# Third norm's mean ahead of its second low parts, turns of the mixed rows four to a slot, high weights first in slots two to four

## The chip, the cores and the metric

The kernel runs on one core of one Trainium2 chip. The metric is the device time of one execution in microseconds (us), lower is better. Before the change it is 2747.4 us (median of three runs, 2747.28 to 2749.04).

## The reference, cut to what matters

256 tokens of width 2048 pass through two blocks, all in float32. The parts of the computation that the change touches:

```python
# start of block one: the first norm feeds the first projection
h = rms_norm(x, mix_pre_g);  proj = h @ w_in          # first columns used: v
# end of block one, start of block two (third norm of the kernel's numbering)
x = x + rms_norm((silu(gate) * up) @ w_ffn_out, ffn_post_g)
h = rms_norm_2(x, norm_mix_pre_2);  z = h @ w_in_2    # first columns used: R0
# block two: the "mixed rows"
gates = sigmoid(gate_logits + b_branch_gates)
mixed = (gates[0] * y_a + gates[1] * (o @ w_branch_b_2)) @ w_out_2
```

## The kernel before, in words

**Two parts of every number.** TensorE multiplies in a reduced float32 form, so every factor is split into a high part (rounded) and a low part (what the rounding left). A product is three matmuls: low tokens times high weights, high tokens times low weights, high times high. Token factors live in `AH`/`AL` and `BH`/`BL` (high/low), the weights of the moment in `RH`/`RL`.

**The weight stream.** The weights come as 964 slots of 128x1024 numbers (512 KB), in the order in which they are used. Slot `i` is loaded by the SP queue into `RAW[i % 4]`; ScalarE copies it to its high part `RH[i % 4]` (line 1166); VectorE subtracts to get the low part `RL[i % 4]` (line 1672); TensorE multiplies with both. Each ring has four places: the high part of slot `i` waits until TensorE is through with slot `i-4`, and the load of slot `i` waits until the low part of slot `i-4` is made. A slot of a product by tokens is 12 matmuls of 512 columns: 2 blocks of 128 input features, 2 halves of the tokens, 3 products. `by_token` writes them; it waits for the slot's low part first (`wait_low`) and then, in the first product that uses new tokens, for the tokens' low parts (`ready`).

**Order of the other work.** Each engine's program is in a fixed order. `upto(i + LA)`, with `LA = 3`, makes the part of slot `i+3` while the engine's program stands at slot `i`. Everything else is a generator that yields the slot at which its next piece is to be written, in halves; `sides.behind(i - 0.5)` and `sides.behind(i)`, behind the part of slot `i+3`, write what is due. So a piece with 3.5 stands behind the part of slot 7 of its count, a piece with 4.5 behind that of slot 8, and what is written later on the same engine waits for it.

**The start.** Slot 0 (`first_slot`) goes by parts: 4 high-high, 4 with low tokens, 4 with low weights. Slots 1 to 7 of the pass `v0` go through `by_token`.

**The third norm** (`n == 3`, pass `R0`). The last product of block one ends by halves of the tokens. In `half_norm` VectorE adds the sum of a half, makes the mean of the squares (`"mean"`, needs ScalarE's squares), GpSimd raises it to the power -1/2, VectorE adds the scaled rows to `X` in quarters (`"first_quarters"` and on). TensorE turns the quarters of `X` (`half_turns`, steps 0 to 7), ScalarE makes the high and VectorE (`half_lows`) the low parts of each step. `by_token_head` mixes these turns with the products of the first four slots of `R0`. Steps 0 and 1 belong to the first half of the tokens, 2 and 3 to the second.

**The mixed rows.** Passes `yb0` to `yb3` (8 slots each) are followed by `W0`, which multiplies the rows that they make. Behind the last slot of each `yb{j}` VectorE takes the product from PSUM (one operation), adds the other branch (one), turns 128x1024 numbers by 16 transposes of 32x256 (line 2151, four for each `fq`); ScalarE makes the high part (`mixed_task`, line 1484), VectorE the low part (`mixed_task`, line 2136 and on). In `W0` the slot numbered 7 from the last of `yb3` is the first to need the low part of `yb3` (`ready` is `(s_ybl, k // 4 + 1)`, two `k` to a slot).

Of the kernel before, what the change touches and what calls it, by code (L numbers as in the profile page):

```python
# [13 lines left out]
P = 128  # L14
# [153 lines left out]
def build(nc, A, out, scratch):  # L168
    ctx = ExitStack()
    with ctx:  # L170
# [87 lines left out]
        def last(name):  # L258
            return groups[name][-1]
# [296 lines left out]

        X_AT = [5, 6, 8, 9]
        X_CHUNK, X_PIECES = [0, 2, 4, 8, 12, 16], [1, 2, 3, 4]
        X_HALF = [(half, b) for half in range(2) for b in range(2)]


# [15 lines left out]
        def tensor(g):  # L577
# [75 lines left out]
            def by_token(name, H, L, ready=None):  # L653


                banks, k = unit[name, 0], 0
                tail = groups[name][-2:] if name == "ckv1" else []
                wait_unit(name)
                for i in groups[name]:
                    if i in tail:  # L660
                        break
                    if i == 0:
                        first_slot(banks, H, L)
                        k = 2
                        sides.behind(i)
                        continue
                    wait_low(i)
                    hi, lo = parts(i)
                    for j in range(2):
                        if ready:  # L670
                            g.wait_ge(*ready(k))
                        end = i == last(name) and j == 1
                        for b in range(2):
                            o, bs = PS[:, banks[b], :], slice(b * P, b * P + P)
                            mm(o, L[:, k, bs], hi[:, j, :], k == 0, False)
                            mm(o, H[:, k, bs], lo[:, j, :], False, False)
                            t = mm(o, H[:, k, bs], hi[:, j, :], False, end)
                        k += 1
                        if j == 0:
                            sides.behind(i - 0.5)  # L680
                    t.then_inc(s_slot, 1)
                    sides.behind(i)
                if tail:
                    for b in range(2):
                        o, bs = PS[:, banks[b], :], slice(b * P, b * P + P)
                        for n, i in enumerate(tail):
                            wait_low(i)
                            hi, lo = parts(i)
                            for j in range(2):
                                c = k + 2 * n + j  # L690
                                mm(o, L[:, c, bs], hi[:, j, :], False, False)
                                mm(o, H[:, c, bs], lo[:, j, :], False, False)
                                t = mm(o, H[:, c, bs], hi[:, j, :], False, n == 1 and j == 1)
                            if b:
                                t.then_inc(s_slot, 1)
                        if b == 0:
                            t.then_inc(s_vh, 1)
# [61 lines left out]
            def by_token_head(name, H, L, n):  # L759

                banks, head = unit[name, 0], groups[name][:4]
                wait_unit(name)

                def highs(b, ms):
                    for m in ms:
                        g.wait_ge(s_nhi, 8 * n + 2 * b + m // 2 + 1)
                        g.wait_ge(s_hi, head[m] + 1)  # L770
                        for j in range(2):
                            mm(PS[:, banks[b], :], H[:, 2 * m + j, b * P:b * P + P], parts(head[m])[0][:, j, :], m + j == 0, False)

                def low_tokens(b, ms):
                    for m in ms:
                        g.wait_ge(s_nlo, 8 * n + 2 * b + m // 2 + 1)
                        for j in range(2):
                            mm(PS[:, banks[b], :], L[:, 2 * m + j, b * P:b * P + P], parts(head[m])[0][:, j, :], False, False)

                def low_weights(b, ms):  # L780
                    for m in ms:
                        wait_low(head[m])
                        for j in range(2):
                            t = mm(PS[:, banks[b], :], H[:, 2 * m + j, b * P:b * P + P], parts(head[m])[1][:, j, :], False, False)
                        if b:
                            t.then_inc(s_slot, 1)
                            sides.behind(head[m])

                highs(0, range(2))
                if n == 3:  # L790
                    low_weights(0, range(2))
                highs(0, range(2, 3))
                low_tokens(0, range(2))
                highs(0, range(3, 4))
                if n == 3:
                    half_turns(n, 2, 3)
                low_tokens(0, range(2, 4))
                if n != 3:
                    half_turns(n, 2, 3)
                    low_weights(0, range(1))  # L800
                half_turns(n, 3, 4)
                if n != 3:
                    low_weights(0, range(1, 2))
                highs(1, range(4))
                low_tokens(1, range(4))
                low_weights(1, range(2))
                half_turns(n, 4, 6)
                low_weights(0, range(2, 4))
                low_weights(1, range(2, 4))
                rest_by_token(name, H, L, n)  # L810
# [350 lines left out]
        def scalar(g):  # L1161
# [321 lines left out]

            def mixed_task():
                for j in range(4):
                    yield last(f"yb{j}") + 3
                    g.wait_ge(s_ybt, j + 1)
                    act(AH[:, 4 * j:4 * j + 4, :], MIXT[j % 2].rearrange("p (c t) -> p c t", c=4)).then_inc(s_ybh, 1)

# [177 lines left out]
        def vector(g):  # L1667
# [74 lines left out]
            def half_norm(n, half):  # L1742


                f = first(NORMED[n])
                for step in ("early", "sum", "mean", "first_quarters"):
                    half(0, step)
                upto(f + (n == 3))
                if n != 3:
                    half(0, "last_gain")  # L1750
                    half(0, "third_quarter")
                    half(0, "last_quarter")
                half(1, "early")
                half(1, "sum")
                half_lows(n, 0, 2)
                if n == 3:
                    half(0, "last_gain")
                half(1, "mean")
                half(1, "first_quarters")
                upto(f + 2)  # L1760
                half_lows(n, 2, 4)
                upto(f + 3)
                if n == 3:
                    half(0, "third_quarter")
                half(1, "third_quarter")
                upto(f + 4)
                half_lows(n, 4, 5)
                half(1, "last_gain")
                if n == 3:
                    half(0, "last_quarter")  # L1770
                half(1, "last_quarter")
                half_lows(n, 5, 6)
                upto(f + 6)
                half_lows(n, 6, 8)
# [361 lines left out]
            def mixed_task():  # L2136

                for j in range(4):
                    z = MIXED[:, 1024 * j:1024 * j + 1024]
                    src = z.rearrange("p (b c d i) -> p b c d i", b=2, c=4, d=4)  # L2140
                    dst = MIXT[j % 2].rearrange("p (c b d i) -> p b c d i", c=4, b=2, d=4)
                    yield last(f"yb{j}") + 0.5
                    g.wait_ge(s_free_v, read_v[f"yb{j}"])
                    tt(z, z, T0[:, 1024 * j:1024 * j + 1024], ALU.add).then_inc(s_yba, 1)
                    g.wait_ge(s_yba, j + 1)
                    if j > 1:
                        g.wait_ge(s_ybl, j - 1)
                    for fq in range(4):
                        yield last(f"yb{j}") + (0.5, 1, 1.5, 2)[fq]
                        for tq in range(4):  # L2150
                            t = g.transpose(dst[32 * fq:32 * fq + 32, :, :, tq, :], src[32 * tq:32 * tq + 32, :, :, fq, :])  # L2151
                    t.then_inc(s_ybt, 1)
                    yield last(f"yb{j}") + 3
                    g.wait_ge(s_ybh, j + 1)
                    tt(AL[:, 4 * j:4 * j + 4, :], MIXT[j % 2].rearrange("p (c t) -> p c t", c=4),
                       AH[:, 4 * j:4 * j + 4, :].bitcast(F32), ALU.subtract).then_inc(s_ybl, 1)
# [514 lines left out]
```

## Time and profile before

| | |
|---|---|
| median of three runs | 2747.4 us |
| the profiled execution's own time | 2747.37 us |
| its span, first to last instruction | 2745.6 us |
| TensorE (PE) busy | 2731.2 us, 99% of the span |
| VectorE (DVE) busy | 1821.2 us, 66% |
| ScalarE (ACT) busy | 1336.2 us, 49% |
| GpSimd (POOL) busy | 58.1 us, 2% |
| chain that ended last, TensorE's share | 97% |
| mean granted clock | 0.999 |

PE is the matmul row, PEld the load of the 128x128 factor that stands still. A matmul's end in the profile is modelled, so two that follow one another overlap in it; the pitch from start to start is the true pace. Idle time stands in brackets with the operation that ended it.

### The profile page before, as it was taken

Reading aid. Unit: us, or ns where it says so; the run is one execution under the profiler, and the core shown is the slowest. Engines: PE = TensorE matmul, PEld = TensorE weight load, DVE = VectorE, ACT = ScalarE, POOL = GpSimd, SP = SyncE. Lnnn points to the kernel's source line nnn. Section 1 sums busy time; section 2 is a strip of 40 time slices with the busy share of each in tenths; the row PEclk is TensorE's granted clock in tenths of the full one; section 3 lists DMA queues with packets and bytes.
Section 4 is the critical chain, followed back from the end, with each engine's and each line's share of the span. In section 5 each row is a group of like instructions: output and inputs, shape, how many; then the busy total and the mean of one; then the engine's idle time right before and its main releaser. Section 6 shows DMA issues by size and latency. Waiting matters only on the chain.

```text
span 2745.6 us, 35317 instructions
## 1 busy us (share of the span) xinstructions
PE 2731.2 (99%) x14290; PEld 2272.1 (83%) x14290; DVE 1821.2 (66%) x2308; ACT 1336.2 (49%) x1606; POOL 58.1 (2%) x57
## 2 busy tenths in 40 slices
PE   9999999999999999999999999999999999999998
PEld 7888888888888888888888888888888888888887
DVE  6778865675556656766678654868667556656675
ACT  6566554654444434445545545544454444444443
POOL 0000000000000000000002000000000000000000
PEclk9999999999999999999999999999999999999999
DMA  9645455566655656555655656665665555565555
GB/s 327 204 160 174 154 192 173 180 206 194 194 192 189 199 194 195 193 185 178 215 173 182 192 178 206 192 214 177 206 197 192 194 192 196 180 206 192 195 189 161
DMA packets 145396, 529.21 MB, mean 193 GB/s; under 512 B 16289, under 2 KB 16721, under 8 KB 144593
## 3 DMA queue, kind: packets, MB, share of 16 engines
q1 hardware_dynamic: 142240, 514.45, 57.4%
q0 software_dynamic: 2560, 12.07, 1.2%
q8 instruction: 113, 1.85, 0.3%
q10 hardware_dynamic: 432, 0.43, 0.1%
q14 instruction: 51, 0.41, 0.0%
HBM read 524.78 MB, written 2.11 MB: 192 GB/s over the span
## 4 chain that ended last, share of the span: by engine, by line
PE 97%; DVE 2%; DMA 0%; issue 0%; ACT 0%; POOL 0%; DVEq 0%; SPq 0%; POOLq 0%
PE PS L580 96%; PE PS L583 1%; DVE AR L2151 1%; DMA RAW<-in_stream 0%; DVE RL L1672 0%; DVE AR L1672 0%; DVE X L1678 0%; DVE A_HL L1678 0%; POOL ST L2437 0%; ACT RH L1166 0%; ACT SP L1166 0%; DVEq L170 0%; ACT A_HL L1166 0%; DVE A_HL L1672 0%; POOLq L170 0%
## 5 line engine op out<-in xcount | busy, mean ns | idle before, releaser
L1672 DVE TENSOR_TENSOR RL<-RAW,RH 128x1024 fp32r<-128x1024 f32 x958 | 1162.9, 1224 | 820.5 <-ACT RH L1166 818.2
L1166 ACT ACTIVATE RH<-RAW 128x1024 fp32r<-128x1024 f32 (+1 forms) x962 | 1013.9, 1057 | 1105.2 <-PE PS L580 1084.2
L580 PE MATMUL PS<-RH,A_HL 128*128 128x512 f32 x4096 | 1265.7, 391 | 2.6 <-DVE RL L1672 1.4
L580 PEld LDWEIGHTS PS<-RH,A_HL 128*128 128x128 f32 x4096 | 767.7, 188 | 165.7 <-ACT A_HL L1166 2.3
L580 PE MATMUL PS<-RH,B_HL 128*128 128x512 f32 x2624 | 808.6, 390 | 0.0
L580 PE MATMUL PS<-RL,A_HL 128*128 128x512 f32 x2048 | 787.4, 390 | 0.2 <-DVE RL L1672 0.2
L580 PEld LDWEIGHTS PS<-RH,B_HL 128*128 128x128 f32 x2624 | 492.3, 188 | 103.0 <-DVE RL L1672 0.5
L580 PE MATMUL PS<-RL,B_HL 128*128 128x512 f32 x1312 | 507.5, 389 | 0.0
L580 PEld LDWEIGHTS PS<-RL,A_HL 128*128 128x128 f32 x2048 | 383.9, 188 | 79.0 <-DVE RL L1672 0.9
L580 PEld LDWEIGHTS PS<-RL,B_HL 128*128 128x128 f32 x1312 | 246.1, 188 | 50.8 <-DVE RL L1672 0.2
L580 PE MATMUL PS<-A_HL,RH 128*128 128x512 f32 (+1 forms) x912 | 219.3, 393 | 0.0
L580 PEld LDWEIGHTS PS<-A_HL,RH 128*128 128x128 f32 (+1 forms) x912 | 165.3, 188 | 33.1 <-issue 1.0
L2127 DVE STREAM_TRANSPOSE AR<-AR 32x256 f32<-32x256 f32 x352 | 153.4, 436 | 4.9
L580 PEld LDWEIGHTS PS<-A_HL,RL 128*128 128x128 f32 (+1 forms) x912 | 117.0, 191 | 6.1 <-issue 0.6
L580 PE MATMUL PS<-A_HL,RL 128*128 128x256 f32 (+1 forms) x912 | 121.8, 286 | 0.0
L1672 DVE TENSOR_TENSOR AR<-PS,AR 128x512 f32<-128x512 f32 (+2 forms) x106 | 77.3, 740 | 46.0 <-ACT AR L1166 28.2
L1672 DVE TENSOR_TENSOR AR<-AR 128x512 f32<-128x512 f32 (+3 forms) x145 | 100.8, 733 | 0.3
L1166 ACT ACTIVATE AR<-AR 128x1024 f32<-128x1024 f32 (+2 forms) x64 | 65.0, 1030 | 15.7 <-DVE AR L1672 11.1
L1166 ACT ACTIVATE AR<-PS,ST 128x512 f32<-128x512 f32 (+1 forms) x74 | 45.6, 664 | 50.9 <-PE PS L580 46.5
L1166 ACT ACTIVATE AR<-PS 128x512 f32<-128x512 f32 (+2 forms) x48 | 31.5, 664 | 73.6 <-PE PS L580 71.3
L2437 POOL TENSOR_TENSOR ST<-ST,NEG 128x1 f32<-128x1 f32 (+2 forms) x21 | 22.5, 1070 | 2022.7 <-DVE ST L1678 1733.3
L580 PEld LDWEIGHTS PS<-AR 128*32 128x32 f32 (+5 forms) x1938 | 48.7, 119 | 13.0 <-issue 8.9
(122 smaller groups left out, 831.5 us busy)
## 6 DMA issues: line engine op xcount, KB each, us to landing
RAW<-in_stream SPq DMA_DIRECT2D x960, 512.0 KB, 4.2
X<-in_x SPq DMA_DIRECT2D x4, 512.0 KB, 7.7
AR<-in_mem SPq DMA_DIRECT2D x4, 512.0 KB, 6.3
AR<-in_mem_turned SPq DMA_DIRECT2D x4, 512.0 KB, 5.8
AR<-in_b_branch_gates POOLq DMA_DIRECT2D x4, 512.0 KB, 6.3
AR<-in_b_branch_gates POOLq DMA_DIRECT2D x2, 1024.0 KB, 8.8
out_x<-X SPq DMA_DIRECT2D x8, 256.0 KB, 2.7
AR<-in_x_turned SPq DMA_DIRECT2D x3, 512.0 KB, 9.2
```

Of the source, the lines that this page charges most:

```text
L580: return g.matmul(o, l, r, start=start, stop=stop, skip_group_check=True)
L583: return g.transpose(o, i, ident)
L1166: return g.activation(o, i, f, bias=bias, scale=scale, accum_out=accum)
L1672: return g.tensor_tensor(o, a, b, f)
L2127: t = g.transpose(dst[32 * fq:32 * fq + 32, :, :, tq, :], src[32 * tq:32 * tq + 32, :, :, fq, :])
L2151: t = g.transpose(dst[32 * fq:32 * fq + 32, :, :, tq, :], src[32 * tq:32 * tq + 32, :, :, fq, :])
L2437: return g.tensor_tensor(o, i, NEG[:, 0:k], ALU.pow)
```

## The change

Three places. First, slots 1, 2 and 3 of the first pass go by parts as slot 0 does: high tokens by high weights, low tokens by high weights, high tokens by low weights, with the wait for the slot's low part only ahead of the third. Second, for the third norm VectorE makes the second half's mean between the low parts of steps 0 and 1 (before: behind both and behind one more product, `"last_gain"` of the first half, which now stands behind the first two quarters); TensorE places the turn of step 2 ahead of the last low-token products instead of ahead of the last two. Third, the 16 transposes of each mixed pass are written four to a slot (before: eight), the high part a slot later, the low part a slot and a half later. For the other norms the order is the same as before, though written differently.

```diff
+        HIGH_FIRST = [1, 2, 3]
...
+                    hi, lo = parts(i)
+                    if i in HIGH_FIRST:
+                        g.wait_ge(s_hi, i + 1)
+                        for low in range(3):
+                            if low == 2:
+                                wait_low(i)
+                            for j in range(2):
+                                if ready and low < 2:
+                                    g.wait_ge(*(ready(k + j) if low else (s_nhi, (k + j) // 2 + 1)))
+                                for b in range(2):
+                                    t = mm(PS[:, banks[b], :], (L if low == 1 else H)[:, k + j, b * P:b * P + P],
+                                           (lo if low == 2 else hi)[:, j, :], False, False)
+                        k += 2
+                        t.then_inc(s_slot, 1)
+                        sides.behind(i)
+                        continue
                     wait_low(i)
-                    hi, lo = parts(i)
...
                 highs(0, range(3, 4))
+                low_tokens(0, range(2, 3 if n == 3 else 4))
+                half_turns(n, 2, 3)
                 if n == 3:
-                    half_turns(n, 2, 3)
-                low_tokens(0, range(2, 4))
-                if n != 3:
-                    half_turns(n, 2, 3)
+                    low_tokens(0, range(3, 4))
+                else:
                     low_weights(0, range(1))
                 half_turns(n, 3, 4)
...
             def mixed_task():            # ScalarE
                 for j in range(4):
-                    yield last(f"yb{j}") + 3
+                    yield last(f"yb{j}") + 4
...
                 half(1, "early")
                 half(1, "sum")
-                half_lows(n, 0, 2)
+                half_lows(n, 0, 1)
+                if n == 3:
+                    half(1, "mean")
+                half_lows(n, 1, 2)
+                if n != 3:
+                    half(1, "mean")
+                half(1, "first_quarters")
                 if n == 3:
                     half(0, "last_gain")
-                half(1, "mean")
-                half(1, "first_quarters")
                 upto(f + 2)
...
                     for fq in range(4):  # VectorE, mixed_task
-                        yield last(f"yb{j}") + (0.5, 1, 1.5, 2)[fq]
+                        yield last(f"yb{j}") + 0.5 + fq
...
-                    yield last(f"yb{j}") + 3
+                    yield last(f"yb{j}") + 4.5
                     g.wait_ge(s_ybh, j + 1)
```

## Rows read from the trace of the kernel before

**Rows 1.** Timeline, TensorE, start: start us, length us, engine, line, operation, [idle before].

```profile
8.94 1.09 PE L580 MATMUL PS<-RL,A_HL 128*128 128x512 f32 x4
10.82 0.50 PE L580 MATMUL PS<-RH,A_HL 128*128 128x512 f32 x1 [0.79 <-DVE RL L1672]
...
11.16 0.40 PE L580 MATMUL PS<-RL,A_HL 128*128 128x512 f32 x1
...
19.33 0.39 PE L580 MATMUL PS<-RL,A_HL 128*128 128x512 f32 x1
```

**Rows 2.** Timeline, ScalarE and VectorE, start: parts of slots 1, 2, 4.

```profile
8.45 1.06 ACT L1166 ACTIVATE RH<-RAW 128x1024 fp32r<-128x1024 f32 x1 [0.31 <-DMA RAW<-in_stream]
...
9.54 1.23 DVE L1672 TENSOR_TENSOR RL<-RAW,RH 128x1024 fp32r<-128x1024 f32 x1 [0.15 <-ACT RH L1166]
...
10.98 1.06 ACT L1166 ACTIVATE RH<-RAW 128x1024 fp32r<-128x1024 f32 x1 [0.37 <-DMA RAW<-in_stream]
...
17.18 1.22 DVE L1672 TENSOR_TENSOR RL<-RAW,RH 128x1024 fp32r<-128x1024 f32 x1 [0.53 <-ACT RH L1166]
```

**Rows 3.** Timeline, TensorE, third norm.

```profile
1275.57 2.17 PE L580 MATMUL PS<-RH,A_HL 128*128 128x512 f32 x8
1279.01 0.63 PE L583 MATMUL PS<-EYE,X 128*128 128x128 f32 x4 [1.27 <-DVE X L1678]
...
1282.22 3.02 PE L580 MATMUL PS<-RH,A_HL 128*128 128x512 f32 x12 [0.16 <-ACT A_HL L1166]
...
1285.99 1.03 PE L583 MATMUL PS<-EYE,X 128*128 128x128 f32 x8
```

**Rows 4.** Timeline, VectorE and (last row) ScalarE, third norm.

```profile
1274.56 2.15 DVE L1678 SCALAR_TENSOR_TENSOR A_HL<-PS,GC,A_HL 128x128 fp32r<-128x128 f32 x8
...
1277.23 0.16 DVE L1678 SCALAR_TENSOR_TENSOR ST<-ST 128x1 f32<-128x1 f32 x1
1278.11 1.42 DVE L1678 SCALAR_TENSOR_TENSOR X<-AR,ST,X 128x512 f32<-128x512 f32 x2 [0.73 <-POOL ST L2437]
...
1284.38 1.41 DVE L1678 SCALAR_TENSOR_TENSOR X<-AR,ST,X 128x512 f32<-128x512 f32 x2
...
1275.69 0.26 ACT L1166 ACTIVATION_READ_ACCUMULATOR SP<-AR 128x1 f32 x1
```

**Rows 5.** Timeline, VectorE, first mixed pass; last row: behind W0's last slot.

```profile
1861.60 1.23 DVE L1672 TENSOR_TENSOR AR<-PS,AR 128x1024 f32<-128x1024 f32 x1 [0.34 <-PE PS L580]
...
1865.17 3.57 DVE L2151 STREAM_TRANSPOSE AR<-AR 32x256 f32<-32x256 f32 x8
1868.75 1.23 DVE L1672 TENSOR_TENSOR RL<-RAW,RH 128x1024 fp32r<-128x1024 f32 x1
1870.01 3.60 DVE L2151 STREAM_TRANSPOSE AR<-AR 32x256 f32<-32x256 f32 x8
1873.64 1.22 DVE L1672 TENSOR_TENSOR RL<-RAW,RH 128x1024 fp32r<-128x1024 f32 x1
1874.79 1.22 DVE L1672 TENSOR_TENSOR A_HL<-AR,A_HL 128x1024 fp32r<-128x1024 f32 x1
...
1949.73 1.41 DVE L1672 TENSOR_TENSOR AR<-PS,AR 128x512 f32<-128x512 f32 x2 [0.34 <-PE PS L580]
```

**Rows 6.** Timeline, ScalarE, first mixed pass.

```profile
1873.64 1.06 ACT L1166 ACTIVATE A_HL<-AR 128x1024 fp32r<-128x1024 f32 x1 [5.49 <-DVE AR L2151]
1874.61 2.94 ACT L1166 ACTIVATE RH<-RAW 128x1024 fp32r<-128x1024 f32 x3
```

**Rows 7.** Timeline, TensorE's loads and matmuls: waits behind the first and fourth pass.

```profile
1874.92 0.19 PEld L580 LDWEIGHTS PS<-RH,B_HL 128*128 128x128 f32 x1 [0.18 <-DVE RL L1672]
...
1941.24 0.50 PE L580 MATMUL PS<-RH,A_HL 128*128 128x512 f32 x1 [0.62 <-DVE RL L1672]
```

**Rows 8.** Last matmul (timeline); stretch 2740.50:2741.00 by engine, granted clock third from last.

```profile
2736.80 0.39 PE L580 MATMUL PS<-RH,A_HL 128*128 128x512 f32 x1
...
2740.50:2741.00 0.50, 0.00 (x0) 0.00 (x0) 0.50 (x2) 0.00 (x0) 0.00 (x0) 0.71 0.00 0
```

## The prediction

> **What bounds the kernel now.** I read the page first: TensorE is busy 99% of the span and holds 97% of the chain that ended last. So the other engines matter only where TensorE waits. I then went through TensorE's timeline for idle time in brackets. In the middle of the kernel only a few places have any, and the three largest are just the ones that the change touches: 0.79 us at the start, ended by the low part of slot 1 [rows 1]; 1.27 us in the third norm, ended by the first added quarter of X, and 0.16 us soon behind it [rows 3]; 0.62 us behind the fourth mixed pass, ended by a weight slot's low part [rows 7]. The reader is to see how small this is: even if all of it went, it would be about 3 us of 2747. Last I read the timelines of ScalarE and VectorE around each place, because all three edits reorder fixed queues, and a queue can become late by more than it was.
>
> The pace: TensorE's matmuls with a low weight factor start at 11.16 and 19.33, the second matmuls of slots 1 and 4, 36 matmuls apart [rows 1], so one matmul takes 0.227 us, a slot of twelve 2.72 us, a pass of eight slots 21.76 us.
>
> **Start: slots 1 to 3 by parts.** No matmul is added; the 12 of each slot change places. The last group of slot 0 starts at 8.94, four matmuls, so slot 1 could start at 8.94 + 0.91 = 9.85. It starts at 10.82, and the second matmul comes 0.34 later instead of 0.23 (11.16 [rows 1]), so its true loss is 1.08. Now only the high part is needed first: 8.45 + 1.06 = 9.51 [rows 2], in time. The low part (9.54 + 1.23 = 10.77) is needed eight matmuls later, at 11.66, in time. Slot 2 starts at 12.57 with its high part there at 12.04 [rows 2]; slot 3 starts at 15.29; slot 4 would start at 18.01. Slot 4 waits for its low part as before, which ends at 17.18 + 1.22 = 18.40 [rows 2]; that row is fed by loads, not by TensorE, so it does not come earlier. Next late is therefore this part. Before, slot 4 started at 19.33 - 0.23 = 19.10; after at 18.43, plus 0.11 for the restart: 18.54. Gain 0.55. The bounds: nothing, if the loads run later than here, and 1.08 if they run earlier. I take 0.55, from the row itself.
>
> **Third norm.** The second half's mean needs ScalarE's squares, read out at 1275.69 + 0.26 = 1275.95 [rows 4]. It ran at 1277.23, since eight low-part operations (2.15 us from 1274.56) and a product stood ahead. With only four of the eight ahead it can run at about 1275.98, some 1.25 earlier. From mean to the first added quarter took 0.88 (1278.11 - 1277.23), so that could be at 1276.86; but the other four low-part operations (about 1.1 us, behind the mean) end near 1277.15, and the addition starts then: 0.96 earlier. TensorE's turn moves from 1279.01 to 1278.05 [rows 3]. Between that turn and the wait at 1282.22 TensorE has two low-token matmuls fewer (they now stand ahead of the turn, in the idle time), 0.45, so the twelve matmuls at 1282.22 move by 1.3 to 1.4. The low-token matmuls ahead of the turn are due at 1275.57 + 8 x 0.227 = 1277.39, and their low parts end near 1277.2: 0.2 us of margin. What is late next is the third quarter of X: it ended at 1284.38 + 1.41 = 1285.79 for a turn at 1285.99 [rows 3, 4]; VectorE's queue moves by only 0.96, TensorE by 1.3, so the margin of 0.2 is used up. The product that stands later costs nothing by itself: it is still one operation in the same queue. Gain 1.0. The bounds: a loss of 0.3 if the margin ahead of the turn fails, a gain of 1.6 (both idle rows with their restarts).
>
> **Mixed rows.** The number of operations is the same again, yet the place in the queues is not. Before, 16 transposes stand behind two weight parts and the low part behind the third. I write VectorE's new queue for one pass, from the operation that takes the product from PSUM (0): the first transpose at 3.57 (1865.17 - 1861.60 [rows 5]); four transposes take 1.79 (half of 3.57, and 1.81 at the later ones); a weight part and the step to a transpose take 1.26 (1870.01 - 1868.75). That gives weight parts at 5.36, 8.41 and 11.48 and transposes at 3.57, 6.62, 9.67 and 12.74, ended at 14.54. ScalarE makes the high part at 14.57, and its next weight part, which is queued behind it, 0.97 later (1874.61 - 1873.64 [rows 6]), ended 16.60. VectorE, idle for 2.1 us, makes the low part of that slot at 16.63 and the low part of the mixed rows at 17.78 (1.15 later, 1874.79 - 1873.64 [rows 5]), ended 19.00. Three more weight parts at 1.14 each bring the next pass's first operation to 22.34. The pass takes TensorE 21.76. So each of three passes leaves VectorE 0.58 later, 1.74 at the fourth, and its low part is ended 19.00 + 1.74 = 20.74 behind the moment at which TensorE ends yb3.
>
> When is it needed? TensorE's loads for the sixth slot stood at 1874.92, a wait of 0.06: without it at 1874.86 - 1861.60 = 13.26 [rows 5, 7]. The seventh slot, which is the first to need the fourth low part, starts 2.72 later, at 15.98. It is 4.76 late, with the step to the matmul and the restart (0.05 and 0.11) 4.9. Part of it may fall already at the weight part at 16.63 + 1.23 of the third pass, due at 18.70 and 1.16 late in its queue: that moves some 0.3 of the wait forward and adds one restart, 0.1: in all 5.0. Against it: the waits of before in this stretch go. Between 1861.60 and 1949.73 there are 88.13 us for four passes of 21.76 (87.04), so 1.09 [rows 5], of which the idle row at 1941.24 is the most. Net +3.9. What is queued behind the waiting high part is ScalarE's next weight part, and for that wait VectorE's low part of the slot and the load on the SP queue that takes its place in the ring.
>
> The bounds: -1.1 if the low part were in time; +5 if a load lands late, since a place in the ring comes free only behind the late weight part. The unseen cost is the step from a weight part to transposes of the second and fourth group: I take the 1.26 of the third; the nearest lower row is 1.15 (part to part), which makes each pass 0.2 shorter and the whole 0.8 cheaper.
> On that step the Trainium skill has a rule (VectorE: DVE Perf Modes, Two Vector instructions with no wait between them): an instruction whose input or output starts in another quarter of the partitions than the last one's is held until the earlier ones have ended. The 1.26 against 1.15 agrees, and by it the added groups are held too, which gives +3.9; without it the part would be +3.1.
>
> **Sum.** The profiled execution took 2747.37 us, as good as the median of 2747.4. 2747.37 - 0.55 - 1.0 + 3.9 = 2749.7. TensorE is the bound everywhere behind these places, so each term stays to the end.
>
> **Rivals.** (a) TensorE's clock falls in the new gap. The last matmul ends at 2737.19, and the clock is 0.71 on the mean of 2740.50 to 2741.00 [rows 8], so it went from 2.4 to 1.2 GHz at about 2740.7, 3.5 us behind it. The new gap is 4.9, less the restart (0.11), less the 0.16 by which a matmul's modelled end (0.39) is over the pitch, less the 0.4 that falls earlier, 4.2 us. Against it: how soon the clock falls is seen here once. Its price is half the time at 1.2 GHz; if it is low for 3.5 us of work (an estimate: as long as its fall took) 1.8, total 2751.5. From 6.3 us of low clock on, the kernel is over 0.2% slower: 2753.
> The Trainium skill (TensorE: Matmul & The Clock Gate, Why this matters for your kernels) says to leave no long gap between bursts of matmuls, or the clock halves; it speaks against this change, and by it the time is this rival's.
> (b) It comes out faster: the fourth low part is ready in time, because the queue is shorter than I sum (the third and later weight parts hidden). It must be 4.8 us earlier than my sum. Then 2747.37 - 0.55 - 1.0 - 1.1 = 2744.7. For it speaks only that VectorE is idle 34% of the span.
> (c) The mixed rows cost as forecast, but the first two parts bring nothing: the loads at the start and the quarters in the norm only move the wait. 2747.37 + 3.9 = 2751.3.
>
> **Chances.** Forecast 0.66 (its own range 2748.8 to 2750.7), (a) 0.14, (b) 0.10, (c) 0.10. The range 2747.9 to 2752.0 leaves out (b) and the far end of (a). 0.2% is 5.5 us, what can be told from no change: faster 0.02 (only beyond (b)), same 0.94, slower 0.04 (long low clock in (a)).
>
> **What would show it.** In the trace after: no idle ahead of slot 1 and a short one (0.1 to 0.3 us, low part of slot 4) near 18.4; the norm's idle row of 1.27 down to 0.1 or less, and a new wait of some 0.2 ahead of the turn of step 4; VectorE's passes 22.3 us apart instead of 21.8; and one idle row of 4 us on TensorE, ended by VectorE's A_HL of line 1672, in the middle of W0. If that row is absent or under 2 us, my forecast is wrong and (b) is right. A granted clock under 1 behind that row shows (a).

## The result and the profile after

The changed kernel takes 2751.29 us (median of 22 runs, 2750.28 to 2751.91) against 2747.34 us (22 runs, 2746.88 to 2749.04). The ratio is 1.0013, 95% interval 1.0007 to 1.0018: slower by some 4 us, which is real and still inside 0.2%. The profiled execution took 2751.41 us, its span is 2749.6 us.

The times of one kernel fall into two groups some 1.1 us apart (before, 2746.88 to 2747.40 and 2747.69 to 2749.04; after, 2750.28 to 2750.84 and 2751.19 to 2751.91), and group against group the loss is 3.4 us.

The place-by-place account comes from three moments that both traces have: the first turn of the third norm, VectorE's first operation of the first mixed pass, and its first operation behind the last slot of W0. First the start and the norm on TensorE, in the timeline of the kernel after (start, length, engine, line, operation, [idle before]). A turn is a transpose by TensorE, the rows with EYE.

```profile
9.06 1.09 PE L581 MATMUL PS<-RL,A_HL 128*128 128x512 f32 x4
9.99 1.98 PE L581 MATMUL PS<-RH,A_HL 128*128 128x512 f32 x8
...
17.24 1.07 PE L581 MATMUL PS<-RL,A_HL 128*128 128x512 f32 x4
18.45 0.50 PE L581 MATMUL PS<-RH,A_HL 128*128 128x512 f32 x1
...
1270.99 1.03 PE L584 MATMUL PS<-EYE,X 128*128 128x128 f32 x8
...
1277.52 0.60 PE L584 MATMUL PS<-EYE,X 128*128 128x128 f32 x4
...
1279.35 4.05 PE L581 MATMUL PS<-RH,A_HL 128*128 128x512 f32 x16 [0.32 <-ACT A_HL L1182]
...
1284.15 1.04 PE L584 MATMUL PS<-EYE,X 128*128 128x128 f32 x8
```

The idle rows at 10.82 [rows 1] and 1279.01 [rows 3] are gone. Slot 1 follows slot 0 without a gap, and the only stop at the start is at 18.45, for the low part of slot 4. The first turn of the norm stood at 1271.51 before, so the start gave 0.52 us:

```profile
1271.51 1.03 PE L583 MATMUL PS<-EYE,X 128*128 128x128 f32 x8
```

The turn of step 4 stood at 1285.99 [rows 3], 1.84 later than now, so the norm gave 1.32 us more. Behind it VectorE in the third norm, and then in the mixed rows, same view:

```profile
1274.05 1.12 DVE L1694 SCALAR_TENSOR_TENSOR A_HL<-PS,GC,A_HL 128x128 fp32r<-128x128 f32 x4
1275.45 0.16 DVE L1694 SCALAR_TENSOR_TENSOR ST<-ST 128x1 f32<-128x1 f32 x1 [0.28 <-ACT SP L1182]
...
1276.56 1.41 DVE L1694 SCALAR_TENSOR_TENSOR X<-AR,ST,X 128x512 f32<-128x512 f32 x2
...
1282.83 1.41 DVE L1694 SCALAR_TENSOR_TENSOR X<-AR,ST,X 128x512 f32<-128x512 f32 x2
...
1859.73 1.23 DVE L1688 TENSOR_TENSOR AR<-PS,AR 128x1024 f32<-128x1024 f32 x1 [0.34 <-PE PS L581]
...
1865.09 1.22 DVE L1688 TENSOR_TENSOR RL<-RAW,RH 128x1024 fp32r<-128x1024 f32 x1
1866.34 1.78 DVE L2171 STREAM_TRANSPOSE AR<-AR 32x256 f32<-32x256 f32 x4
...
1882.01 1.21 DVE L1688 TENSOR_TENSOR AR<-PS,AR 128x1024 f32<-128x1024 f32 x1
...
1904.25 1.21 DVE L1688 TENSOR_TENSOR AR<-PS,AR 128x1024 f32<-128x1024 f32 x1
...
1926.47 1.22 DVE L1688 TENSOR_TENSOR AR<-PS,AR 128x1024 f32<-128x1024 f32 x1
...
1943.02 1.22 DVE L1688 TENSOR_TENSOR RL<-RAW,RH 128x1024 fp32r<-128x1024 f32 x1 [2.07 <-ACT RH L1182]
1944.16 1.22 DVE L1688 TENSOR_TENSOR A_HL<-AR,A_HL 128x1024 fp32r<-128x1024 f32 x1
...
1953.80 1.41 DVE L1688 TENSOR_TENSOR AR<-PS,AR 128x512 f32<-128x512 f32 x2 [0.40 <-PE PS L581]
```

The four passes begin 22.28, 22.24 and 22.22 us apart, where TensorE needs 21.76, and the fourth low part ends at 1945.38. From 1859.73 to 1953.80 there are 94.07 us; four passes are 87.04, so 7.03 us more than the work at full clock, against 1.09 before [rows 5]. What TensorE did there, and then the stretches with the granted clock (third from last):

```profile
1941.01 0.39 PE L581 MATMUL PS<-RH,A_HL 128*128 128x512 f32 x1
1945.52 0.76 PE L581 MATMUL PS<-RH,A_HL 128*128 128x512 f32 x1 [4.12 <-DVE A_HL L1688]
1946.09 0.63 PE L581 MATMUL PS<-RL,A_HL 128*128 128x512 f32 x1
...
1947.37 0.63 PE L581 MATMUL PS<-RL,A_HL 128*128 128x512 f32 x1
...
1951.07 0.39 PE L581 MATMUL PS<-RL,A_HL 128*128 128x512 f32 x1
```

```profile
1943.00:1944.00 1.00, 0.00 (x0) 0.00 (x0) 0.98 (x1) 1.00 (x2) 0.00 (x0) 1.00 0.00 0
1944.00:1945.00 1.00, 0.00 (x0) 0.00 (x0) 1.00 (x2) 0.88 (x1) 0.00 (x0) 0.53 0.00 0
...
1946.00:1950.00 4.00, 4.00 (x11) 3.03 (x10) 1.65 (x2) 0.00 (x0) 0.00 (x0) 0.50 0.75 244
1950.00:1951.00 1.00, 1.00 (x4) 0.80 (x3) 0.00 (x0) 0.00 (x0) 0.00 (x0) 0.55 0.74 262
1951.00:1952.00 1.00, 1.00 (x6) 0.78 (x6) 0.00 (x0) 0.92 (x1) 0.00 (x0) 1.00 0.17 70
```

One idle row of 4.12 us, ended by VectorE's low part of the mixed rows. Inside it, at about 1944.06, the clock goes from 2.4 to 1.2 GHz, and it comes back at about 1950.9. Thirteen matmuls from 1945.52 to 1951.07 take 5.55 us; at full clock they take 13 x 0.227 + 0.11 = 3.06. So the clock costs 2.49 us in this execution, and the waits are 7.03 - 2.49 = 4.54 us. The account: 2747.37 - 0.52 - 1.32 + (7.03 - 1.09) = 2751.47, for 2751.41 measured.

### The profile page after: what moved, and what is told of

The parts are those of the page before. It is cut to its first block, busy times and chain, and to the rows that moved or that the text cites. A ratio compares the mean times of both kernels' runs of the same rounds, so it can differ in the third digit from the quotient of the medians.

```text
span 2749.6 us, 35317 instructions
## 1 busy us (share of the span) xinstructions
PE 2733.1 (99%) x14290; PEld 2274.3 (83%) x14290; DVE 1820.6 (66%) x2308; ACT 1335.7 (49%) x1606; POOL 58.0 (2%) x57
## 4 chain that ended last, share of the span: by engine, by line
PE 98%; DVE 1%; DMA 0%; issue 0%; ACT 0%; POOL 0%; DVEq 0%; POOLq 0%; ACTq 0%
PE PS L581 97%; PE PS L584 1%; DMA RAW<-in_stream 0%; DVE RL L1688 0%; DVE X L1694 0%; DMA AR<-in_x_turned 0%; ACT RH L1182 0%; ACT A_HL L1182 0%; DVE A_HL L1694 0%; DVE AR L1688 0%; POOL ST L2457 0%; ACT SP L1182 0%; DVEq L170 0%; DVE A_HL L1688 0%; POOLq L170 0%
```

## The experiments

Two theories stood at the end of the reading. Mine: the three parts are independent, and the loss has two prices, a wait set by VectorE's order and matmuls at half clock behind it. The rivals: gains that are given back later, loads as the cause, the amount of transposing as the cause, something other than the clock behind the gap. All medians are of 11 runs, and beside each stands the median of the kernel before on the same chip. The interval of one such comparison is about 2.5 us to either side, so differences of a few tenths are read from traces, and the medians only agree or do not.

**mixed_only.** The kernel before with only the third part (the last two hunks of the diff and the one in ScalarE's `mixed_task`).

> The kernel before with the third part of the change alone (mixed rows four turns to a slot). Theory: this part holds the whole loss, +3.4 us of waiting behind VectorE's queue and +1.3 to +2.5 us of matmuls at 1.2 GHz behind the wait, so 2752.0 to 2753.3 us, with one idle row of about 4.1 us in W0. Rival (the loss belongs to a later start of the loads, or to the three parts together): under 2750.5 us here.

2753.03 us against 2747.81: +5.2, interval 1.0011 to 1.0029. TensorE's timeline has the same idle row:

```profile
1947.37 0.76 PE L580 MATMUL PS<-RH,A_HL 128*128 128x512 f32 x1 [4.14 <-DVE A_HL L1672]
```

This part alone holds the loss. The clock fell here too, but eight matmuls behind the gap, from 1947.37 to 1950.77, take 3.40 us for 8 x 0.227 + 0.11 = 1.93 at full clock: the price is 1.5 us in this trace, not 2.5.

**start_norm.** The changed kernel with the third part undone.

```diff
-                    yield last(f"yb{j}") + 4         # ScalarE
+                    yield last(f"yb{j}") + 3
...
-                        yield last(f"yb{j}") + 0.5 + fq
+                        yield last(f"yb{j}") + (0.5, 1, 1.5, 2)[fq]
...
-                    yield last(f"yb{j}") + 4.5       # VectorE
+                    yield last(f"yb{j}") + 3
```

> The changed kernel with the third part undone: by the theory the gains of the first two parts stay to the end, 2747.34 - 0.5 - 1.3 = 2745.5 us, no idle row over 1 us outside the end. Rival (an earlier TensorE only waits later): 2746.5 to 2747.4 us.

2745.56 against 2747.81: -2.25, interval 0.9985 to 1.0002, which just holds no change; the 1.8 of the two traces lies in it. One expectation failed: there is an idle row over 1 us, at 1940.13 behind the fourth mixed pass (1.17 us, ended by a weight slot's low part). It is the wait of [rows 7], longer here since a load kept ScalarE waiting for 3.47 us at 1924.63. That wait is part of the old order, not of the new gains.

**start_only** and **norm_only.** The first part alone on the kernel before; the second part alone (the list of slots empty).

```diff
-        HIGH_FIRST = [1, 2, 3]
+        HIGH_FIRST = []            # norm_only, with the third part undone too
```

> The kernel before with slots 1 to 3 by parts alone. Theory: -0.5 us, 2746.8 us; the idle of 0.79 us ahead of slot 1 goes, and slot 4 waits for its low part at about 18.4 us. Rival (the gain is given back in the slots behind): 2747.3 us.

2747.47 against 2747.81: -0.3 by the medians, with an interval that holds no change (0.9990 to 1.0008). The trace tells it better: the norm's first turn at 1271.11 instead of 1271.51.

> The kernel before with the third norm's part alone (the branch for slots 1 to 3 is there but used for none). Theory: -1.3 us, 2746.0 us; the idle of 1.27 us goes, a wait of 0.3 us for ScalarE's high parts stays. Rival, as forecast (the third quarter of X is late by 0.2): -1.0 us, 2746.3 us, with a wait ahead of the turn of step 4.

2746.56 against 2747.81: -1.25, interval 0.9987 to 1.0005. From the first turn to that of step 4 there are 1284.73 - 1271.60 = 13.13 us, against 14.48 before: 1.35. No wait stands ahead of step 4. The sum of the three parts alone, -0.3 - 1.25 + 5.2 = +3.6, is about the whole, +3.95. Nothing in these medians shows one part taking from another, though their intervals would hide a few tenths.

**fill12.** Work without use in the gap, so that the wait stays and TensorE does not stand still.

```diff
+        FILL = 12
...
+                        if name == "W0" and k == 12:
+                            g.wait_ge(s_free_v, read_v["yb3"])
+                            for _ in range(FILL):
+                                mm(PS[:, unit["W1", 0][_ % 2], :], H[:, 0, 0:P], hi[:, 0, :], True, False)
                         if ready:
                             g.wait_ge(*ready(k))
```

> The changed kernel with 12 more matmuls (2.72 us at full clock) in W0, written into two banks that the next pass starts anew, just ahead of the wait for the fourth mixed low part: work without use that fills the gap and moves no other engine. Theory (two prices, the wait and the clock): the wait still ends when VectorE is done, so the time falls only by the clock's price, 1.3 to 2.5 us, to 2748.8 to 2750.0 us; the idle row is 1.4 us and the granted clock stays 1.00 behind it. Rival (the slow matmuls behind the gap are another thing): 2751.3 us or up to 2754.0 us, clock low as before.

2749.62 against 2747.70: +1.9, where the changed kernel has +3.95. More matmuls, less time. TensorE's timeline and the stretches:

```profile
1942.23 3.11 PE L582 MATMUL PS<-RH,A_HL 128*128 128x512 f32 x13
1946.66 0.50 PE L582 MATMUL PS<-RH,A_HL 128*128 128x512 f32 x1 [1.32 <-DVE A_HL L1693]
1947.00 0.40 PE L582 MATMUL PS<-RL,A_HL 128*128 128x512 f32 x1
```

```profile
1946.00:1948.00 2.00, 1.34 (x6) 1.10 (x7) 2.00 (x3) 0.10 (x1) 0.00 (x0) 1.00 0.74 252
1948.00:1950.00 2.00, 2.00 (x10) 1.64 (x9) 0.87 (x1) 0.18 (x1) 0.00 (x0) 1.00 0.55 195
```

The wait ends as before, with VectorE's low part; the clock stays at 2.4 GHz and the pitch behind the gap is the usual one. VectorE's first operation of the first mixed pass stands at 1860.95 and the one behind W0 at 1952.47, 91.52 us, which is 4.48 over the 87.04 of work: the waits of the changed kernel (4.54) are all there, and its 2.49 for the clock are gone. So the second price is the clock. By the medians, 3.95 against 1.92, it is 2.0 us.

**fourth_alone.** Only the fourth pass in the new order.

```diff
-                    yield last(f"yb{j}") + 4
+                    yield last(f"yb{j}") + (3, 3, 3, 4)[j]
...
-                        yield last(f"yb{j}") + 0.5 + fq
+                        yield last(f"yb{j}") + ((0.5, 1, 1.5, 2)[fq] if j < 3 else 0.5 + fq)
...
-                    yield last(f"yb{j}") + 4.5
+                    yield last(f"yb{j}") + (3, 3, 3, 4.5)[j]
```

> The changed kernel with the first three mixed passes as before and only the fourth four turns to a slot. Theory (two sources of the wait: the late place of the low part, 19.0 against 16.0 us, and the drift of 0.5 us a pass): the gap goes from 4.5 to 3.1 us, or 4.0 us if a load lands late as in the kernel before; 2747.7 to 2748.6 us if the clock stays, up to 2.5 us more if it falls. Rival (the drift is all of it): 2745.5 us, no gap.

2750.88 against 2747.70, runs of 2748.20 to 2751.94, and none near the 2745.5 of the rival. The drift is not all of it: TensorE's row is

```profile
1946.37 0.76 PE L581 MATMUL PS<-RH,A_HL 128*128 128x512 f32 x1 [3.83 <-DVE A_HL L1688]
```

which is the upper of the two cases: a load was late again (VectorE idle 2.82 us at 1926.19). The clock fell inside this gap too, to 0.50 from about 1946.0. Seven matmuls from 1946.37 to 1949.46 take 3.09 us for 1.70 at full clock, a price of 1.4 us. But this trace does not show the late place by itself. The late load put VectorE's first operation of the fourth pass at 1927.33, 1927.33 - 1860.64 - 65.28 = 1.41 us behind three of TensorE's passes, as much as the drift did in the changed kernel (1926.47 - 1859.73 - 65.28 = 1.46). So place and late load together lose the clock here. Whether the place alone would, with the gap of 3.1 us that was expected then, is not shown; two of the 11 runs, 2748.20 and 2748.33, lie where a kept clock was expected, and they have no trace.

**low_ahead.** VectorE's low part half a slot earlier.

```diff
-                    yield last(f"yb{j}") + 4.5
+                    yield last(f"yb{j}") + 4
```

> The changed kernel with VectorE's low part of the mixed rows half a slot earlier (4 in place of 4.5), so that it stands ahead of the eighth slot's weight part. Theory: it falls into the 2.1 us in which VectorE stood idle, ends at 16.9 us instead of 19.0, and a pass takes VectorE 21.3 us, no drift: a wait of about 1 us is left, 2745.5 us, clock 1.00. Rival (VectorE's transposes four to a slot are too much work in any order): 2748 us or more.

2745.39 against 2747.70: -2.3, interval 0.9983 to 1.0000, no loss left. VectorE's timeline:

```profile
1937.68 1.80 DVE L2171 STREAM_TRANSPOSE AR<-AR 32x256 f32<-32x256 f32 x4
1940.61 1.23 DVE L1688 TENSOR_TENSOR A_HL<-AR,A_HL 128x1024 fp32r<-128x1024 f32 x1 [1.13 <-ACT A_HL L1182]
1941.75 3.48 DVE L1688 TENSOR_TENSOR RL<-RAW,RH 128x1024 fp32r<-128x1024 f32 x3
```

The idle time of 2.07 us at 1943.02 is down to 1.13, the low part ends 16.9 us behind the pass instead of 18.9, and TensorE waits 0.74 us, with the clock at 1.00 behind it. The passes begin 21.76 us apart (1859.67, 1881.43, 1903.19, 1924.95), so the drift is gone too. The same transposes in the same groups: their amount is not the cause, the place of one operation is.

**three_groups.** low_ahead with the transposes 8, 4 and 4 besides.

```diff
-                        yield last(f"yb{j}") + 0.5 + fq
+                        yield last(f"yb{j}") + (0.5, 0.5, 1.5, 2.5)[fq]
```

> As low_ahead, with the transposes in groups of 8, 4 and 4 (at 0.5, 1.5 and 2.5). Theory: transposes end at 13.3 us behind yb3, the low part of the seventh slot at 14.5, the mixed low part at 15.6, ahead of the 16.0 at which TensorE needs it: no wait in any pass, 1.1 us less than before in this stretch, 2744.4 us. Rival (loads that come in bursts set a wait of their own here): 2745.3 us.

2744.53 against 2747.70: -3.2 (ratio 0.9989, 0.9980 to 0.9998). Behind the third norm no idle row stands in TensorE's timeline up to its last matmul, though a load was late here too (ScalarE waited 2.43 us for it at 1923.97). VectorE's part and the mixed low part stand without idle time between:

```profile
1937.63 1.80 DVE L2171 STREAM_TRANSPOSE AR<-AR 32x256 f32<-32x256 f32 x4
1939.45 1.23 DVE L1688 TENSOR_TENSOR RL<-RAW,RH 128x1024 fp32r<-128x1024 f32 x1
1940.59 1.22 DVE L1688 TENSOR_TENSOR A_HL<-AR,A_HL 128x1024 fp32r<-128x1024 f32 x1
```

**three_groups_start1** and **three_groups_start4.** three_groups with `HIGH_FIRST = [1]` and `[1, 2, 3, 4]` in place of `[1, 2, 3]`.

> As three_groups, with only slot 1 by parts (slots 2 and 3 as before the change). Theory (slots 2 and 3 keep what slot 1 gains): slot 2 would start at 12.6 us and waits for its low part of 13.3 us, so most of the gain of 0.55 us is lost: 0.35 us slower than three_groups. Rival (slot 1 alone matters): the same time as three_groups.

2744.78 against 2747.53: 0.25 over three_groups, which ran on another chip, or 0.4 when each is taken against its own runs of before. The row behind slot 1 is the wait that was expected:

```profile
13.29 0.50 PE L581 MATMUL PS<-RH,A_HL 128*128 128x512 f32 x1 [0.50 <-DVE RL L1688]
```

> As three_groups, with slot 4 by parts too. Theory (what is left late at the start is slot 4's low part at 18.4 us, needed at 18.0): its wait goes, 0.5 us faster than three_groups. Rival (the loads are late behind it): the same time.

2743.89 against 2747.53, ratio 0.9987 (0.9978 to 0.9996): 0.9 below start1 on the same chip and 0.6 below three_groups (0.5 when each is taken against its own runs of before). Slot 4 now follows at once,

```profile
17.98 1.98 PE L581 MATMUL PS<-RH,A_HL 128*128 128x512 f32 x8
```

so slot 4's low part was what was late at the start. This version is the fastest: 3.6 us below the kernel before and, each taken against its own runs of before (-3.64 and +3.95), 7.6 below the changed one.

**turn_as_before.** three_groups with TensorE's order in the norm as before, VectorE's as changed.

```diff
-                low_tokens(0, range(2, 3 if n == 3 else 4))
-                half_turns(n, 2, 3)
                 if n == 3:
-                    low_tokens(0, range(3, 4))
-                else:
+                    half_turns(n, 2, 3)
+                low_tokens(0, range(2, 4))
+                if n != 3:
+                    half_turns(n, 2, 3)
                     low_weights(0, range(1))
```

> As three_groups, with TensorE's order in the third norm as before the change (turn of step 2 ahead of both pairs of low-token matmuls) and VectorE's order as changed. Theory (nearly all of the norm's gain is VectorE's earlier mean): 0.3 us slower than three_groups, as two matmuls less lie in the idle time ahead of the turn. Rival (TensorE's order holds the gain): 1 us or more slower.

2744.90 against 2747.53, 0.4 over three_groups (0.5 against their own runs of before). From the first turn to that of step 4 there are 1285.30 - 1271.87 = 13.43 us against 1285.11 - 1271.98 = 13.13 in three_groups, with an idle row ahead of step 2:

```profile
1278.33 0.63 PE L584 MATMUL PS<-EYE,X 128*128 128x128 f32 x4 [0.24 <-DVE X L1694]
```

So TensorE's move holds 0.3 us of the norm's 1.35, and VectorE's changed order (the mean earlier, `last_gain` later) the rest; these two were not tried apart.

## Why the prediction was right, and where not

The direction, the place, the engine and the range held: 2751.3 lies in 2747.9 to 2752.0. The likeliest case did not come out: its sum of 2749.7 puts the clock at nothing, and rival (a), given 0.14, is what happened. That this rival's 2751.5 is so near the measured 2751.3 is in part luck. In the traces the norm gave 0.3 more and the mixed rows cost 0.45 less than forecast, and the clock cost 0.7 more than (a) had, so the errors cancel.

- **Start, forecast -0.55, measured -0.52.** Low part of slot 4 at 18.45, as forecast from [rows 2]. three_groups_start4 shows it to be the limit.
- **Third norm, forecast -1.0, measured -1.32 to -1.35.** The mean came 1.8 us earlier in time (1275.45 against 1277.23), 1.26 of it beyond what the start gave, for the forecast 1.25, and the turn of step 2 came 0.97 earlier beyond it (1277.52 against 1279.01), for the forecast 0.96. The step that failed is "the third quarter of X is late next". The turn of step 4 takes the two halves of the tokens one after the other, with a wait for each (`half_turns`), so at its start it needs only the first of the two additions: 1282.83 and half of 1.41 is 1283.5, and the turn is at 1284.15. I had put the end of both against the start of the turn. The wait ahead of step 4 does not exist.
- **Mixed rows, forecast +3.9, measured +3.45 without the clock.** VectorE's pass was forecast at 22.34 and is 22.25 in the mean, the low part ended 18.91 behind its pass (forecast 19.00), and late by 1945.38 - 1859.73 - 65.28 = 20.37 (forecast 20.74). The queue written out by hand was right to 0.1 us a pass; three passes and the end make the 0.4. The wait at the third pass's weight part, forecast at 0.3 and a restart of 0.1, is small: the gap in W0 is 1945.52 - 1941.01 - 0.227 + 0.11 = 4.39 of the 4.54, which leaves 0.15 for it. It shows on TensorE's weight loads alone, where the one at 1922.07 stood idle for 0.24 us, ended by a weight slot's low part.
- **The added groups' step, taken at 1.26.** Measured 1866.34 - 1865.09 = 1.25 at the second group and 1.26 at the third and fourth. By the Trainium skill's rule on held instructions (VectorE: DVE Perf Modes, Two Vector instructions with no wait between them) the added groups are held as the old one was; this trace agrees. No run here separates the change of quarter from the change from subtraction to transpose, so the reason of the step is the skill's and not shown.
- **Clock, left out of the sum; price forecast in (a) 1.8, measured 2.49, 1.5 and 1.4.** This is the step of the likeliest case that failed. The one fall in the rows came 3.5 us behind the last matmul [rows 8], and the forecast gap of 4.2 (4.12 in the trace) is longer than that. So the rows spoke for (a), and the only reason against it was that they showed one fall; 0.14 was too low. The price depends on how long the clock stays low. In this execution that was 5.4 us of work for the 3.5 I had taken, in mixed_only and fourth_alone 3.2 and 3.0. Nor does it seem to be 5.4 in every run of the changed kernel: the mean granted clock is 0.999 in the nine fastest of the 22 and 0.998 in 11 of the other 13. The Trainium skill's warning (TensorE: Matmul & The Clock Gate, Why this matters for your kernels) agrees with this trace: behind the gap of 4.12 us the granted clock is 0.50.
- **Rival (b), no gap,** is refuted by the row at 1945.52; **rival (c), the first parts bring nothing,** by the moments of the trace: the 0.52 and the 1.32 are still there some 575 us later, at VectorE's first operation of the mixed rows, 1859.73 against 1861.60. The median of start_norm agrees.

With the terms as measured the same sum gives 2747.37 - 0.52 - 1.32 + 3.45 + 2.49 = 2751.47.

## What to carry to other kernels

Spreading an operation over more steps of a fixed queue makes it finish later, and what stands at its end moves behind work that has nothing to do with it: write the queue out with starts and ends, compare its total with the period of the engine that bounds, and compare its last result with the moment of its first use. A low part that is put behind a hand-over to another engine belongs directly behind that hand-over, not behind the next regular piece. And a long gap on TensorE is to be priced twice, once as the wait and once as the slow matmuls behind it: the gaps of 3.83, 4.12 and 4.14 us here cost 1.4 to 2.5 us besides the wait, while those of 0.74 (low_ahead), 1.17 (start_norm) and 1.32 (fill12) left the clock at 1.00. What lies between was not tried.

## What was not expected of the hardware

- The clock's fall is not at a fixed distance. It came 3.5 us behind the end of the last matmul at the end of the kernel before, about 2.7 us behind it in the kernel after (1941.40 to 1944.06), 3.9 in mixed_only (1943.23 to 1947.16) and 3.4 in fourth_alone (1942.55 to 1946.0). The work at low clock behind it was 5.4 us in the kernel after, 3.2 us in mixed_only and 3.0 us in fourth_alone. What sets these was not tried.
- In fill12 and fourth_alone the first eight matmuls of slot 0 stand 0.44 us apart instead of 0.25, which is the pace at 1.2 GHz, while the row of the granted clock says 1.00 there:

```profile
7.06 3.74 PE L582 MATMUL PS<-RH,A_HL 128*128 128x512 f32 x8 [0.90 <-ACT RH L1187]
```

  Both traces are 1.1 us later from there on (305.92 and 305.84 against 304.77 at the same matmuls), as much as the distance between the two groups in which the times of one kernel fall. So such a start can be one part of the scatter of some 1 us. It is not the only one: the trace of three_groups (2745.36, of its upper group) starts at the usual pace and is late by a wait for a weight slot's low part at 585.04 (0.55 us idle), so that its norm begins at 1271.98 for 1271.04 in low_ahead. The account above pairs a trace of the lower group (2747.37) with one of the upper (2751.41), so the whole of its 4.0 us is not the loss of every run.
